# Value tiles in three parts inside the indexer, gate products ahead of the last value tiles

## What is computed

```
h = rmsnorm(x)
aq, ak, av, ag, iq, ik, iw, bq, bk, bv, bg, blr = split(h @ even_w_in)
# A: sparse attention: an indexer scores every key, the best 256 keys are kept
score = sum_head iw_h * relu(iq_h . ik) / 8        -> causal mask, top-k per query
a_out = softmax(aq . ak / 8 + bias, kept keys) @ av   * silu(ag)
# B: gated linear attention in chunks of 64 tokens
log_a = log_sigmoid(blr @ gate_w2 + gate_b2) / 16
G = cumsum(log_a) within a chunk
q_dec = q exp(G), k_dec = k exp(-G), k_tail = k exp(G_last - G)
o = tril(q_dec . k_dec) @ bv + q_dec @ S;  S = exp(G_last) S + k_tail^T @ bv
g_out = head_rmsnorm(o) * silu(bg)
x = x + rmsnorm([a_out, g_out] @ even_w_out)
```

## Time and profile before

| | us |
|---|---|
| median of 3 runs | 1117.87 (1117.31 to 1119.39) |
| profiled execution, its own time | 1114.39 |
| its span, first to last instruction | 1112.6 |
| busy: TensorE | 1011.4 (91%) |
| busy: VectorE | 689.8 (62%) |
| busy: ScalarE | 458.0 (41%) |
| busy: GpSimd | 268.1 (24%) |

### The profile page before, as it was taken

How to read it: one execution, slowest core, us unless ns; L and a number is a source line. 1 busy time by engine, 2 the same in 40 slices (tenths; PEclk the granted TensorE clock), 3 DMA queues, 4 the chain that set the end, 5 groups by cost and what they waited for, 6 DMA issues and landing times.

```text
span 1112.6 us, 14632 instructions
## 1 busy us (share of the span) xinstructions
PE 1011.4 (91%) x5642; PEld 815.4 (73%) x5642; DVE 689.8 (62%) x1220; ACT 458.0 (41%) x780; POOL 268.1 (24%) x199
## 2 busy tenths in 40 slices
PE   4996889989999999789999778989999999895997
PEld 3885679968877776557777566878788888684885
DVE  5314679997779597874554462574539393967042
ACT  6323552253422323335555563433246363573031
POOL 2210212102332322313131564120313122124000
PEclk8998999989999999899999898999999999997999
DMA  7251102101112223101010434322211121112052
GB/s 242 63 71 38 39 1 77 39 1 38 57 56 87 76 67 114 40 25 43 16 53 24 156 106 154 111 75 76 81 52 57 38 57 39 38 38 92 22 189 75
DMA packets 71738, 75.81 MB, mean 68 GB/s; under 512 B 5064, under 2 KB 58360, under 8 KB 71672
## 3 DMA queue, kind: packets, MB, share of 16 engines
q1 hardware_dynamic: 70400, 73.30, 21.1%
q10 hardware_dynamic: 1272, 1.62, 1.3%
HBM read 58.13 MB, written 16.25 MB: 67 GB/s over the span
## 4 chain that ended last, share of the span: by engine, by line
PE 76%; DVE 13%; ACT 5%; issue 4%; POOL 1%; DMA 1%; DVEq 0%; SPq 0%; POOLq 0%; ACTq 0%
PE ps L1588 21%; PE ps L1590 20%; PE ps L1589 20%; PE ps L1833 2%; PE ps L1817 2%; PE ps L1676 2%; PE ps L1768 1%; DVE prob L1370 1%; PE ps L1678 1%; PE ps L1765 1%; PE ps L1677 1%; ACT relu L861 1%; DVE ysL L1525 1%; PE ps L1736 1%; DVE y L1517 1%
## 5 line engine op out<-in xcount | busy, mean ns | idle before, releaser
L1588 PE MATMUL ps<-hH,wH 128*128 128x512 f32 x384 | 159.1, 414 | 15.5 <-DVE qkL L1358 10.0
L1228 DVE TENSOR_SCALAR_CACHE_REDUCE junk<-score,cand 128x384 bf16<-128x384 f32 (+2 forms) x192 | 169.7, 942 | 1.3
L1590 PE MATMUL ps<-hH,wL 128*128 128x512 f32 x384 | 152.7, 398 | 0.0
L1589 PE MATMUL ps<-hL,wH 128*128 128x512 f32 x384 | 152.3, 397 | 0.0
L612 POOL TENSOR_TENSOR wL<-raw,wH 128x1024 fp32r<-128x1024 f32 x32 | 77.1, 2413 | 157.3 <-ACT wH L768 157.3
L1588 PE MATMUL ps<-h1H,w_slot_H 128*128 128x512 f32 x256 | 100.4, 392 | 2.5 <-DVE h1L L1472 2.5
L1590 PE MATMUL ps<-h1H,w_slot_L 128*128 128x512 f32 x256 | 100.3, 392 | 0.0
L1589 PE MATMUL ps<-h1L,w_slot_H 128*128 128x512 f32 x256 | 100.2, 391 | 0.0
L1588 PEld LDWEIGHTS ps<-hH,wH 128*128 128x128 f32 x384 | 73.6, 192 | 35.3 <-issue 21.3
L1590 PEld LDWEIGHTS ps<-hH,wL 128*128 128x128 f32 x384 | 73.6, 192 | 16.2
L1589 PEld LDWEIGHTS ps<-hL,wH 128*128 128x128 f32 x384 | 73.9, 192 | 13.3
(11 more groups left out here) (242 smaller groups left out, 2266.7 us busy)
## 6 DMA issues: line engine op xcount, KB each, us to landing
raw<-in_even_w_in SPq DMA_DIRECT2D x32, 512.0 KB, 4.0
xt<-in_x SPq DMA_DIRECT2D x16, 512.0 KB, 5.6
raw<-in_odd_w_in SPq DMA_DIRECT2D x16, 512.0 KB, 3.9
gate_d<-gst SPq DMA_DIRECT2D x16, 256.0 KB, 2.2
raw_row<-in_even_w_out SPq DMA_DIRECT2D x8, 512.0 KB, 3.4
x_d<-xt SPq DMA_DIRECT2D x8, 512.0 KB, 2.6
raw_row<-in_odd_w_out SPq DMA_DIRECT2D x8, 512.0 KB, 3.2
xt<-x_d SPq DMA_DIRECT2D x8, 512.0 KB, 4.7
```

The costliest lines, as they stand in the source:

```text
L1228: return steps(dve.tensor_scalar(junk1[:, j % 3, 0:(qb + 1) * P], score_of(qb), threshold, None, op, ALU.add, accum_out=dst[:, j:j + 1]))
L1588: pe.matmul(dst, lH, rH, start=k == 0, stop=False)
L1589: pe.matmul(dst, lH, rL, start=False, stop=False)
L1590: return pe.matmul(dst, lL, rH, start=False, stop=k == nk - 1)
```

## The change

Three edits on the same stretch, from the indexer to GLA:
- In the indexer a part of an av0 tile follows every score pair: steps 0 to 2, 3 to 5 and 6 to 7 of the eight, where a whole tile stood behind every third pair.
- The gate products stand between the tiles of bv0 and bv1 and write to banks 2 to 5 without a wait for a bank; ACT takes them out ahead of bv1's values, and Abs, Exp and Ln of both pairs stand one by one behind the first six of these evictions, into buffers of their own (`g_n0`, `g_n1`). POOL's constants stay behind the last tile of bv1. `exponents` stand behind the first and the third bqk product.
- The places of DVE's steps: `gates_summed(0)` at n = 20 (was 24), `keys_decayed(0)` and `gates_summed(1)` at 26 (28), `keys_decayed(1)` at 31 (32), `gla_step(t)` at 36 + 7t//2 (34 + 3t).

```
-    PRODUCTS += [(name, i, t) for name in ("av", "bv") for i in range(2) for t in range(NT)]
+    PRODUCTS += [(name, i, t) for name, i in (("av", 0), ("av", 1), ("bv", 0)) for t in range(NT)]
     PRODUCTS += [("gate", pr, hf) for pr in range(2) for hf in range(2)]
+    PRODUCTS += [("bv", 1, t) for t in range(NT)]
...
+    def GATE_BANK(pr, hf):
+        return 2 + 2 * pr + hf
...
-        pool.wait_ge(proj_full, nth_product("gate", 0, 0))
+        pool.wait_ge(proj_full, nth_product("bqk", BQK_ORDER[0], 0))
...
+        for pr, g_l in ((0, g_a), (1, kdec[:, 1, :])):
+            for hf in range(2):
+                act.wait_ge(proj_full, nth_product("gate", pr, hf) + 1)
+                act.activation(g_l[:, hf * HALF:(hf + 1) * HALF], ps[:, GATE_BANK(pr, hf), :], ACT.Identity,
+                               bias=b2[:, pr:pr + 1]).then_inc(proj_copied, 1)
+        act.wait_ge(proj_copied, copy_count("gate", 1, 1))
         for t in range(NT):
             values_out("bv", 1, t)
+            if t == 0:
+                own(act.activation(g_n0[:, :], g_a[:, :], ACT.Abs))
+            if t == 1:
+                own(act.activation(g_n1[:, :], kdec[:, 1, :], ACT.Abs))
+            if t == 2:
+                own(act.activation(g_n0[:, :], g_n0[:, :], ACT.Exp, scale=-1.0))
+            if t == 3:
+                own(act.activation(g_n1[:, :], g_n1[:, :], ACT.Exp, scale=-1.0))
+            if t == 4:
+                act.activation(g_n0[:, :], g_n0[:, :], ACT.Ln, bias=onet).then_inc(ln_ready, 1)
+            if t == 5:
+                act.activation(g_n1[:, :], g_n1[:, :], ACT.Ln, bias=onet).then_inc(ln_ready, 1)
...
-            if n % 2:
+            if n % 2 == 0:
                 exponents(n // 2)
...
-            if n == 24:
+            if n == 20:
                 dve.wait_ge(gla_const, 1)
                 gates_summed(0)
-            if n == 28:
+            if n == 26:
                 keys_decayed(0)
                 gates_summed(1)
-            if n == 32:
+            if n == 31:
                 keys_decayed(1)
             for t in range(NT):
-                if n == 34 + 3 * t:
+                if n == 36 + 7 * t // 2:
                     gla_step(t)
...
+        for n in range(len(QBS) * PAIRS):
+            head_scores(QBS[n // PAIRS], n % PAIRS)
+            token_tile("av", 0, n // 3, range(3 * (n % 3), min(3 * (n % 3) + 3, KD)))
+        for t in range(NT):
+            token_tile("av", 1, t)
+        pe.wait_ge(acc_done, len(QBS) * A_HEADS)
+        for t in range(NT):
+            token_tile("bv", 0, t)
         rank_rows = slice(IW_BLR_AT, IW_BLR_AT + RANK)
...
+                pe.matmul(ps[:, GATE_BANK(pr, hf), :], w2[rank_rows, pr, :], iwblr[rank_rows, hf * HALF:(hf + 1) * HALF],
                           start=True, stop=True).then_inc(proj_full, 1)
+        for t in range(NT):
+            token_tile("bv", 1, t)
```

More of the change, by code:

```diff
@@ L168, in build @@
     g_b = at("g_b", [P, T], F32, R2 + 32 * KB)
-    g_b1 = at("g_b1", [P, T], F32, R2 + 36 * KB)
+    g_n0 = at("g_n0", [P, T], F32, R1 + 44 * KB)
+    g_n1 = at("g_n1", [P, T], F32, R1 + 40 * KB)
     g_c = at("g_c", [P, T], F32, R2 + 20 * KB)
@@ L1243, in gates_summed @@
             dve.wait_ge(ln_ready, pr + 1)
-            g_l, g_n = ((g_a, g_b), (kdec[:, 1, :], g_b1))[pr]
+            g_l, g_n = ((g_a, g_n0), (kdec[:, 1, :], g_n1))[pr]
             own(dve.scalar_tensor_tensor(g_l[:, :], g_l[:, :], 0.0, g_n[:, :], ALU.min, ALU.subtract))
@@ L1601, in bank_free @@
             key = PRODUCTS[q - 2]
+            if key[0] == "gate":
+                key = PRODUCTS[q - 2 - 4]
             if key[0] in BY_DVE:
@@ L1612, in column_half, with token_tile @@
             weights_first(q % 2, (wH[:, s], wL[:, s]), hf).then_inc(proj_full, 1)
-        def token_tile(name, i, t):
+        def token_tile(name, i, t, ks=range(KD)):
             c = {"av": C_AV, "bv": C_BV}[name] + 2 * i
             slot, q = dst_slot(c), nth_product(name, i, t)
-            pe.wait_ge(w_lo, c + 2)
-            bank_free(q)
+            if ks[0] == 0:
+                pe.wait_ge(w_lo, c + 2)
+                bank_free(q)
             toks = slice(t * P, (t + 1) * P)
-            for k in range(KD):
+            for k in ks:
                 last = three(ps[:, q % 2, 0:NEAR], (hH[:, k, toks], hL[:, k, toks]),
                              (wH[:, slot:slot + 2, k, :], wL[:, slot:slot + 2, k, :]), k, KD)
-            last.then_inc(proj_full, 1)
+            if ks[-1] == KD - 1:
+                last.then_inc(proj_full, 1)
         pe.wait_ge(w2_in, 48)
@@ L1712, in _ @@
             for hf in range(2):
-                q = nth_product("gate", pr, hf)
-                bank_free(q)
-                pe.matmul(ps[:, q % 2, :], w2[rank_rows, pr, :], iwblr[rank_rows, hf * HALF:(hf + 1) * HALF],
+                pe.matmul(ps[:, GATE_BANK(pr, hf), :], w2[rank_rows, pr, :], iwblr[rank_rows, hf * HALF:(hf + 1) * HALF],
                           start=True, stop=True).then_inc(proj_full, 1)
+        for t in range(NT):
+            token_tile("bv", 1, t)
         for n, i in enumerate(BQK_ORDER):
```

## The result

| | before | after |
|---|---|---|
| median of 20 runs each, us | 1116.89 (1114.20 to 1120.34) | 1122.74 (1113.37 to 1123.91) |
| ratio, 95% interval | | 1.0036 (1.0020 to 1.0052) |
| profiled execution, its span, us | 1112.6 | 1119.8 |
| first logits of the attention, us | 434.87 | 439.73 |

The change makes the kernel slower by about 4 us by the ratio (2.2 to 5.8 by its interval); the medians differ by 5.9, since the runs of the changed kernel lie in groups (see e8). The forecast was no change, +0.6 us, with slower as the likeliest sign. The gains came as forecast and a little larger; what takes them back was mis-sized.

A forecast was written before the change was run, and what follows sets the result against it. TensorE (PE) was taken to set the time until 434.9 us; 10 + 8.1 - 8.9 - 2.0 - 0.9 - 5.4 - 1.5 = -0.6 made the profiled 1114.39 into 1115.0, as median 1118.5, own range 1112 to 1123.

The forecast's parts named there:

- Part 1: Indexer: value tiles in thirds cover PE's waits for the relu; PE gains about 10 us, bounds 8.5 and 12.
- The two deductions: Indexer: little DVE slack, and an accumulation about 1.9 us too long beside POOL; 11.8 us of gain taken as 10.
- Part 2: Gate products in front of bqk: PE gains 8.1 us, from the 5.46 us wait and 2.6 us of lower clock.
- Part 3 up to n = 20: DVE's counts before the first gate sums: collisions with POOL cost 3.2 and 0.3 us; DVE there at b + 5.4.
- Part 3 to the second turn: From gate sums to first copy_predicated: DVE at b + 68.3, PE at b + 62.0; wait taken as 8.9 us with collisions.
- b: PE's start of the bqk products, counted in us from its start of the av1 tiles; forecast 73.0.
- rival 2: Slower, DVE's chain rules: second key decay later than b + 53.0, first turn waits 4.9 us; 1125 us, chance 0.22.
- The fourth turn: GLA turn at i = 6, which needs DVE's copy of n = 43: PE waits 0.9 us.
- The sixth: GLA turn at i = 9, needing DVE's copy of n = 50: wait 1.6 us, 5.4 more if a settle is caught.
- the clock: Lower PE clock behind waits at the GLA turns: 2.0 us lost behind the first wait, 1.5 behind the last.
- Rivals 1 and 3: GLA turns: 1, few collisions, 1111 or 1108 us, chance 0.27; 3, PE never waits for DVE's copies, 1100, 0.03.
- The tie to the whole time: From the attention's start at 434.9 us to the end: a shift there is carried to the end unchanged.

The follow-up runs named there:

- e8: The changed kernel without an edit, profiled once more; one run, 1123.46 us.
- e1: The changed kernel with all DVE steps back at their old places (n = 24, 28, 32, 34 + 3t); 1105.89 us, ratio to before 0.9909.
- e5: The changed kernel with DVE steps at n = 20, 25, 30 and 34 + 3t; 1102.44 us, ratio to before 0.9896.
- e6: The changed kernel with GpSimd's low parts of chunks 10, 11, 14 and 16 cut to one column each; 1118.41 us, ratio to before 1.0024.
- e11: The changed kernel with only the GLA steps back at 34 + 3t (others at n = 20, 26, 31); 1101.02 us, ratio to before 0.9858.
- e4: The kernel before with the new DVE places alone (n = 20, 26, 31, 36 + 7t//2); 1136.79 us, ratio to before 1.0155.
- e3: The changed kernel with whole av0 tiles and the old DVE places, leaving the gates in front; 1113.87 us, ratio to before 0.9975.
- e2: The kernel before with the av0 tiles in thirds alone; 1105.65 us, ratio to before 0.9889.
- e9: e4 with PE's waits at the second, fourth and sixth turn filled with 28, 3 and 35 matmuls nobody reads; ratio to before 1.0153.
- e12: The changed kernel with GLA steps at 36 + 3t (others at n = 20, 26, 31); 1107.49 us, ratio to before 0.9898.

## Why the prediction was right or wrong

The measured median, 1122.74, is inside the forecast's own range (to 1123) by 0.3 us. The mechanism, PE waiting for DVE's copies behind collisions, is the one that ran; the sum is less good than the number, because errors of both signs met in it.

**Part 1**: 12.0 us against 10 taken, at the upper bound of 12. The two deductions did not come true; only three waits for a relu are left, 1.8 us in all. DVE's lag behind the start of av1 is 3.4 us (153.19 less 149.8), as forecast.

**Part 2**: 8.1, as forecast, in the profile. In five others part of it went again, because the clock fell behind the gate products: in e8 (0.72 from 196 to 208 us) bv1's first eviction came 3.1 us later behind the one before it than in the profile of after, in e1, e5, e6 and e11 (0.79 from 196 to 204 us) 1.5 us later. The forecast had no price for that.

**Part 3 up to n = 20**: right. The settle of the third round met the pair of low parts (1.07 + 2.31 us) and the next lost 0.3; DVE began the gate sums at 227.98, 5.3 us behind PE's start of bqk at 222.65, forecast 5.4.

**Part 3 to the second turn**: the copy ended at b + 73.3 (295.98). Forecast was b + 68.3 and 5.2 us of possible collisions, of which I took 2.7; practically all came (2.1, 2.0 and 1.0 us at 235, 259 and 285). This is rival 2's condition: the second key decay ended at b + 57.1, where its limit was b + 53.0, and the first turn waited 3.9 us, forecast for rival 2 as 4.9. So one sign of being right, no wait over 1.2 us before 285 us, was missed in this profile, and the wait at the second turn was 3.2 instead of 6 to 9 us. In e8 the decay ended at b + 51.7, the first turn did not wait and the second waited 6.8. The two turns together lost 14.4 us in the profile, forecast 10.9 with the clock.

**The fourth turn**: 0.9 forecast, 0.91 measured. **The sixth**: 1.6, and 5.4 more if a settle is caught, was forecast; the profile has 1.53 without it, e8 8.38 with it, 1.4 more than the 7.0 of the sum. The mechanism was right, with both ends. The sum took 5.4 as the mean of the two, which neither execution had.

**The term that was mis-sized is the clock**: 3.5 us for both waits. The profile of after has 15 (4.1, 3.2, 1.7, 4.5 and 1.5), of which the first 4.1 probably only shortened the wait at the second turn: DVE's copy, for which PE waits there, came no earlier for it. e4 and e8 show it in the cleaner form: 2.8 us behind a wait of 6.8 and 5.7 behind 8.4. I had one price from the trace of before, 2.6 us behind 5.46, took 2.0 and 1.5 from it for waits of 8.9 and 5.4 us, and put nothing behind the short wait at the fourth turn; waits of 1.61 (e3) and 1.53 us cost 3.2 and 4.5 more. The sum by the measured terms: 19.9 - 14.4 - 2.6 - 6.0 - 1.5 = -4.6, beside the -4.9 of the first logits; with e8's, 15.5 - 9.6 - 1.0 - 14.1 = -9.2, beside -9.3. In the profile the gains were thus 1.8 us larger than in the forecast and the waits 5.6 smaller (9.6 for 15.2), while the lower clock cost 11.7 more (15.2 for 3.5): that the median stayed in the range is in part luck. e8 has the forecast's course, no wait at the first turn and long ones at the second and sixth; the first profile begins like rival 2, but without its long wait later. Rivals 1 and 3 are not what these traces show.

**The tie to the whole time**: "I carry a shift at 434.9 to the end unchanged" was off by 2.3 us in the profiled pair (4.9 to 7.2 in the spans), and by up to 2.9 in the other profiles (e2); in the changed kernel the clock was 0.93 from 435 to 707 us where it had been 0.96 from 430 to 700.

**One premise was misread**: "still idle for 1.45 us at 434.04" is the second low part of the query and key pairs; the first followed the last count at 431.90 without a wait. Before the change DVE thus had no idle time left behind its counts; its spare time lay in its waits for PE inside the GLA steps, 21.5 us between 290 and 434 us.

The Trainium skill, SBUF — State Buffer, "Who interferes with whom", says that an instruction caught by the shared ports is blocked for the whole of the other. The settles agree: those that issued just behind a GpSimd operation of 2.35 to 2.40 us took 2.25 to 2.33 us instead of 0.17 and ended with it. The Trainium skill, TensorE: Matmul & The Clock Gate, "Why this matters for your kernels", warns of idle gaps between bursts of matmuls. e9 agrees for the second and sixth turn, whose clock stayed at 1.00 once the gaps were filled; at 388 us of the changed kernel (0.66) and at 328 us of e9 (0.58) it fell without a gap, and there the measurement decides.

## What to carry to other kernels

When an engine has a long queue of filler work (the counts) with steps for another engine at fixed places, moving the producer ahead means moving the steps ahead too, or leaving them; here the GLA steps were moved back and further apart, and the filler was done 11 us too early while PE waited. Check where the filler ends: idle time of the helper behind its last piece is a sign that its steps stand too late. Cost a wait of TensorE at itself plus the lower clock behind it, which here was anything from 0.1 to 5.7 us, and look at two executions before you believe how two engines that block each other meet. A loss ahead of the first edited step, as between e11 and e12, belongs to the execution and not to the edit.

## What was not expected of the hardware

- The clock fell without a wait of PE: 3.2 us lost in e2 (windows below, PE is busy throughout) and e9, 1.5 or 1.6 in e5, e9 and the changed kernel; e11 lost 1.5 at 304 us, some 18 us behind its only wait. No run here shows what made it fall.

```profile
360.00:372.00 12.00, 11.88 (x65) 1.00 0.12 45
372.00:380.00 8.00, 8.00 (x28) 0.57 0.36 97
```

- Collisions make a helper's position discrete: in e4, e6 and e8 the waits agree to 0.02 us (6.76, 6.77, 6.77; 0.91, 0.89, 0.89; 8.37, 8.37, 8.38), though DVE's first copy stands at 310.8, 290.2 and 295.2 us.
- A wait of 0.9 us was followed by 1.7 us of lower-clock loss in one profile of the changed kernel and by 0.1 in the other.
